# Retrieval layers: from gathered expert rows to streaming both expert tables through TensorE

## What is computed

```python
def one_block(xb):                                    # xb: 128 tokens
    q = (xb @ w_q).reshape(n, 8, 2, 128)
    s = jnp.einsum('thpk,pnk->thpn', q, sub_keys)     # 2 x 128 scores a head
    s_top, i_top = lax.top_k(s, 16)
    cand_s = s_top[:, :, 0, :, None] + s_top[:, :, 1, None, :]
    cand_i = i_top[:, :, 0, :, None] * 128 + i_top[:, :, 1, None, :]
    best_s, best_pos = lax.top_k(cand_s.reshape(n, 8, -1), 16)
    idx = jnp.take_along_axis(cand_i.reshape(n, 8, -1), best_pos, axis=-1)
    gate = jax.nn.softmax(best_s, axis=-1)
    act = jax.nn.gelu(jnp.einsum('thkd,td->thk', jnp.take(down, idx, axis=0), xb))
    return jnp.einsum('thk,thkd->td', gate * act, jnp.take(up, idx, axis=0))
```

## Time and profile before

| | us |
|---|---|
| median of 3 runs | 2358.21 (2356.95 to 2359.39) |
| span of the profiled execution | 2356.5 |
| retrieval layer 0 (about 209 to 892) | 683 |
| retrieval layer 1 with the pooling before it (892 to 1587) | 695 |
| rest after it | 769 |
| busy: PE 2048.2, DVE 1155.2, ACT 647.4, POOL 601.8 | |
| moved | 860.93 MB, of it 536.90 MB by gathers |

### The profile page before, as it was taken

One profiled execution on the slowest core, in us unless ns is written; L12 is line 12 of the kernel. 1 busy time (PEld: TensorE's weight loads), 2 busy tenths in 40 slices (PEclk: granted clock), 3 DMA queues, 4 the chain that ended last, 5 costly groups with the idle time before them and its releaser, 6 DMA issues.

```text
span 2356.5 us, 21481 instructions
## 1 busy us (share of the span) xinstructions
PE 2048.2 (87%) x7609; PEld 981.8 (42%) x7609; DVE 1155.2 (49%) x2857; ACT 647.4 (27%) x1813; POOL 601.8 (26%) x516
## 2 busy tenths in 40 slices
PE   7999998777777888998777777779999999999998
PEld 3455664232323336664223223334445544444443
DVE  2335766676667556766676667544534311111111
ACT  2242333332333222333332333332432210000001
POOL 0001344444444431344444444430000000000000
PEclk9999999999999998999999999999999999999999
DMA  9696999999999987999999999996313399999996
GB/s 391 252 423 246 407 417 420 420 416 422 406 420 413 409 347 293 406 420 421 421 420 417 412 421 412 407 396 262 119 57 135 160 402 427 428 426 428 427 427 262
DMA packets 98201, 860.93 MB, mean 365 GB/s; under 512 B 11406, under 2 KB 11534, under 8 KB 12844
## 3 DMA queue, kind: packets, MB, share of 16 engines
q0 software_dynamic: 73728, 536.90, 55.3%
q1 hardware_dynamic: 24364, 322.62, 32.9%
HBM read 858.44 MB, written 1.05 MB: 365 GB/s over the span
## 4 chain that ended last, share of the span: by engine, by line
PE 55%; DMA 29%; DVE 7%; ACT 4%; issue 3%; POOL 2%; POOLq 0%; SPq 0%; DVEq 0%; ACTq 0%
DMA arena<-in_experts,arena 16%; PE bank L2348 16%; PE bank L2012 15%; DMA ring<-in_experts,arena 9%; PE bank L2699 9%; PE bank L2745 4%; PE bank L2709 2%; PE bank L2116 2%; DVE arena L1479 2%; DMA arena<-in_w_up 2%; ACT arena L903 2%; POOL arena L696 1%; PE bank L2128 1%; POOL ring L696 1%; DVE ring L1479 1%
## 5 line engine op out<-in xcount | busy, mean ns | idle before, releaser
L2348 PE MATMUL bank<-arena 128*128 128x512 f32 x1040 | 486.3, 612 | 128.6 <-ACT arena L903 128.6
L2348 PE MATMUL bank<-ring,arena 128*128 128x512 f32 x1008 | 472.1, 612 | 116.5 <-ACT arena L903 116.4
L696 POOL DMA_INDIRECT arena<-in_experts,arena x260 | 299.8, 1153 | 638.2 <-PE bank L2348 331.7
L1479 DVE SCALAR_TENSOR_TENSOR arena<-arena,h 128x1024 f32<-128x1024 f32 x260 | 318.7, 1226 | 231.1 <-DMA arena<-in_experts,arena 230.1
L1479 DVE SCALAR_TENSOR_TENSOR ring<-ring,h 128x1024 f32<-128x1024 f32 x252 | 308.9, 1226 | 217.0 <-DMA ring<-in_experts,arena 216.4
L696 POOL DMA_INDIRECT ring<-in_experts,arena x252 | 301.8, 1198 | 329.5 <-PE bank L2348 288.4
L2348 PEld LDWEIGHTS bank<-arena 128*128 128x128 f32 x1040 | 191.2, 193 | 401.6 <-ACT arena L903 201.4
L2348 PEld LDWEIGHTS bank<-ring,arena 128*128 128x128 f32 x1008 | 185.5, 193 | 384.2 <-ACT arena L903 193.9
L894 ACT ACTIVATE arena<-arena 128x2 f32<-128x2 f32 x256 | 52.1, 203 | 838.5 <-DVE arena L1479 456.1
L2699 PE MATMUL bank<-ring,arena 128*64 128x512 f32 x768 | 223.4, 592 | 2.0 <-ACT arena L1096 1.2
L903 ACT ACTIVATE arena<-const,arena 128x128 f32<-128x128 f32 x512 | 177.6, 394 | 8.4
(11 more groups left out here) (430 smaller groups left out, 1811.8 us busy)
## 6 DMA issues: line engine op xcount, KB each, us to landing
ring<-in_w_gate SPq DMA_DIRECT2D x32, 2048.0 KB, 14.8
ring<-in_mod_w SPq DMA_DIRECT2D x20, 2048.0 KB, 11.8
arena<-in_w_up SPq DMA_DIRECT2D x16, 2048.0 KB, 20.9
arena<-in_w_down SPq DMA_DIRECT2D x16, 2048.0 KB, 15.8
ring<-in_w_up SPq DMA_DIRECT2D x16, 2048.0 KB, 16.4
ring<-in_w_down SPq DMA_DIRECT2D x16, 2048.0 KB, 11.5
ring<-in_w_in SPq DMA_DIRECT2D x9, 2048.0 KB, 7.3
ring<-in_peer_w_q SPq DMA_DIRECT2D x8, 2048.0 KB, 12.3
```

What stands on the lines that cost most here:

```text
L696: pool.indirect_dma_start(out=gslot(l, n), out_offset=None, in_=a["experts"], in_offset=bass.IndirectOffsetOnAxis(ap=idx_all[:, t, at:at + ...
L1479: ins = v.scalar_tensor_tensor(out=row, in0=row, scalar=1.0, in1=h[:, t], op0=ALU.mult, op1=ALU.mult, accum_out=act[:, t, HEAD * hh + k:HE ...
L2348: ins = pe.matmul(bank[2 * t + c][:, :], diag[:, PER * (j % 2) + k], row[:, 512 * c:512 * c + 512], start=j % (GROUPS // NT) == 0 and k == ...
```

## The change

Gathers, dot products and diagonals go. Each layer streams both tables whole, in pieces of 1 MB (`PIECE` x 128 partitions), with `down` laid out on the host so that it serves as stationary operand. For each key pair j the kept tile `kept(j)` is [i on partitions, 256 tokens]: PE makes all 128 x 256 products of experts (i, j) with all tokens (`products`, two keys a piece), and ACT writes their gelu there. DVE selects as before, but keeps i, j and the gate's exponent (`picks`); after both tiles' softmax PE turns them to [pick, token]. For each token then `one_hots` writes the one-hot of i (128 wide) and the one-hot of j times gate (64 wide, one half of the keys at a time) over the 128 picks, `spread_gates` multiplies them on PE into the gate matrix [i, j] of that token, 8 tokens a group, and `weigh` multiplies the kept tiles by it in place. `sums` multiplies the kept tiles, as stationary operand, with the streamed `up` rows into banks 0 to 3.

Only 112 of 128 kept tiles have room. So the order of a layer is: 56 pairs of products, with the queries of two heads each ahead of pairs 0, 4, 10 and 17 and the first half's 32 groups spread from pair 33; then 8 times one pair of sums and one of products; then the other sums, with the second half's groups behind pairs 8 to 31 and the last 8 pairs done first for tile 0 and then for tile 1. Pieces come through three places that free when PE has used the third before; the last five have places of their own. The late modulation rows (16 to 19) all go into layer 0, behind pairs 6, 9, 12 and 15, and the modulation totals behind the sums of pair 33 and on. Both tiles' norms stand ahead of a layer's first query, and the first three loads of `w_in_2` go out during layer 1's sums. `win` is kept apart from the constants, slots of later weights move (`MOE_RING`), and POOL has no work. The core of the diff:

```diff
-PER = 2
-GROUPS = PICKS * NT // PER
+TILE = 256
+KEPT = 112
+PAIR_TILES = KEYS // 2
+KEPT_PAIRS = KEPT // 2
+WRAPPED = PAIR_TILES - KEPT_PAIRS
+TAIL = 8
+STREAMS = 3
+PIECE = 2048
+QUERY_AT = {0: 0, 4: 1, 10: 2, 17: 3}
+ROW_AT_PAIR = {6: 16, 9: 17, 12: 18, 15: 19}
...
+EXP_AT = {29: 0, 32: 1}
+TURN_PICKS_AT = {31: 0, 34: 1}
+SPREAD = KEPT_PAIRS - 33
+GROUPS_AT = {33 + p: tuple(range(GROUPS * p // SPREAD, GROUPS * (p + 1) // SPREAD)) for p in range(SPREAD)}
+GROUPS_BEHIND = {p: tuple(range(4 * (p - WRAPPED) // 3, 4 * (p - WRAPPED + 1) // 3)) for p in range(WRAPPED, PAIR_TILES // 2)}
+TOTAL_AT = [{33 + n: n for n in range(10)}, {33: 10, 34: 11}]
...
-                    pool.indirect_dma_start(
-                        out=gslot(l, n), out_offset=None, in_=a["experts"],
-                        in_offset=bass.IndirectOffsetOnAxis(ap=idx_all[:, t, at:at + 1], axis=0)).then_inc(
-                        S[f"gathered{place_of(n)}"], 16)
...
+                def products_out(p):
+                    act_.wait_ge(S["piece_done"], done(l, "d", p))
+                    act_.activation(kept_pair(p), bank[4 + p % 2][:, :], ACT.Gelu_apprx_tanh).then_inc(S["s_ev"], 1)
...
+                def one_hots(half, g):
+                    n = group_no(l, half, g)
+                    at = slice(GROUP * g, GROUP * g + GROUP)
+                    keys = cst("iota")[:, HALF_KEYS * half:HALF_KEYS * half + HALF_KEYS]
+                    if half == 0 and g in (0, GROUPS // NT):
+                        v.wait_ge(S["picks_ev"], NT * l + g // (GROUPS // NT) + 1)
+                    if n >= 2:
+                        v.wait_ge(S["g_done"], n - 1)
+                    i_hot, j_hot = hot_i[:, n % 2], hot_j[:, n % 2]
+                    link(v.tensor_tensor(j_hot, bc(keys, 1, GROUP), bc(picksT[:, 1, at], 2, HALF_KEYS), ALU.is_equal))
+                    v.tensor_tensor(i_hot, bc(cst("iota"), 1, GROUP), bc(picksT[:, 0, at], 2, KEYS), ALU.is_equal)
+                    v.tensor_tensor(j_hot, j_hot, bc(picksT[:, 2, at], 2, HALF_KEYS), ALU.mult).then_inc(S["hot_made"], 1)
...
+                    for at, v0, width in runs:
+                        part = kept_run(v0, width)[:, :, GROUP * g:GROUP * g + GROUP]
+                        ins = v.tensor_tensor(part, part, gates_of_keys[:, at:at + width], ALU.mult)
+                    ins.then_inc(S["w_made"], 1)
...
+                def products(p):
+                    wait_piece(pe, l, "d", p)
+                    if p >= 2:
+                        pe.wait_ge(S["s_ev"], PAIR_TILES * l + p - 1)
+                    w = piece(l, "d", p).rearrange("p (j k n) -> p j k n", j=2, k=KT)
+                    for j in range(2):
+                        ins = accumulate(bank[4 + p % 2][:, TILE * j:TILE * j + TILE], [(w[:, j, q], hT[:, q, :]) for q in range(KT)])
+                    ins.then_inc(S["piece_done"], 1)
...
+                    for u in range(GROUP):
+                        ins = pe.matmul(bank[6 + n % 2][:, HALF_KEYS * u:HALF_KEYS * u + HALF_KEYS], hot_i[:, n % 2, u], hot_j[:, n % 2, u],
+                                        start=True, stop=True)
+                    ins.then_inc(S["g_done"], 1)
...
+                def sums(p, *tiles):
+                    w = piece(l, "u", p).rearrange("p (j d) -> p j d", j=2)
+                    for j in (2 * p, 2 * p + 1):
+                        for t in tiles:
+                            for c in range(2):
+                                ins = pe.matmul(bank[2 * t + c][:, :], tile(kept(j), t), w[:, j % 2, 512 * c:512 * c + 512],
+                                                start=j == 0, stop=j == KEYS - 1, skip_group_check=True)
+                    return ins
```

More of the change, by code:

```diff
@@ L75 @@
 INC = [(0, 512), (512, 512), (1024, 512), (1536, 256)]
+HEAD_QUERIES = [(256 * c, 256) for c in range(HEADS)]
 FIRST = (0, 2, 1, 3)
@@ L118 @@
 OPERANDS = {"tq1": 2, "pctx": 2, "tk1": 1, "ppool": 8, "tkc": 2, "th1": 1, "tq2": 4, "tgla": 3, "tkd": 2, "tgo": 2}
-SHADOW = 4
-STEPS = 15
-ROWS = 18
+STEPS = 14
 GAIN_ROW = 20
[L125 to L132, removed]
@@ L135, in selections @@
-def selections(l, m, head=1):
-    return 9 * l + (m + 1 if m else head) + 1
-PER = 2
-GROUPS = PICKS * NT // PER
-EARLY_SLOTS = 6
-def place_of(n):
[L149 to L159, removed]
+LATE_ROWS = (16, 17, 18, 19)
+TILE = 256
[3 more added lines that the diff above has]
+WRAPPED = PAIR_TILES - KEPT_PAIRS
@@ L482, in program @@
         mo = Carve(0)
-        w_moe = [ring[:, i, :] for i in range(RING)] + [mo(SLOT) for _ in range(2)]
-        moe_landed = w_landed + [S[f"moe_landed{i}"] for i in range(RING, 6)]
-        streamed = [16 * sum(load is not None and k == i for load, k in zip(loads, slots)) for i in range(RING)] + [0, 0]
+        MOE_RING = (2, 1, 0, 3)
+        w_moe = [ring[:, i, :] for i in MOE_RING] + [mo(SLOT) for _ in range(2)]
+        moe_landed = [w_landed[i] for i in MOE_RING] + arena_landed[3:5]
+        streamed = [16 * sum(load is not None and k == i for load, k in zip(loads, slots)) for i in MOE_RING] + [16 * 2, 16 * 2]
         hdn = mo(4, T)
@@ new lines, in peer @@
+                for n in range(HEADS):
+                    for step in range(STEPS):
+                        top_k(n, step)
+                    if l == 0 and n == 4:
+                        v.wait_ge(S["modp"], 4 + 20)
+                        v.tensor_tensor(mrows2, mrows1, bank[3][:, :], ALU.add).then_inc(S["rows_made"], 1)
+                gates(0)
+                for half in range(2):
+                    for g in range(GROUPS):
+                        one_hots(half, g)
+                        if (half, g) == (0, 1):
+                            gates(1)
+                        if g:
+                            weigh(half, g - 1)
+                    weigh(half, GROUPS - 1)
@@ new lines, in query @@
+                def query(hh):
+                    wait_piece(pe, l, "q", hh)
+                    if hh < 2:
+                        pe.wait_ge(S["turned_ev"], turned(tag, 4))
+                    else:
+                        pe.wait_ge(S["pq_ev"], HEADS * l + hh - 1)
+                    w = piece(l, "q", hh).rearrange("p (k n) -> p k n", k=KT)
+                    for half in range(2):
+                        ins = accumulate(bank[hh % 2][:, 256 * half:256 * half + 256],
+                                         [(tile(w[:, q], half), hT[:, q, :]) for q in range(KT)])
+                    ins.then_inc(S["piece_done"], 1)
@@ new lines, in scores @@
+                def scores(n):
+                    c, t = n // 2, n % 2
+                    if l == 0 and n == 1:
+                        pe.wait_ge(S["rows_made"], 2)
+                    pe.wait_ge(S["pq_ev"], HEADS * l + 2 * c + 2)
+                    if n >= 2:
+                        pe.wait_ge(S["ps_ev"], HEADS * l + n - 1)
+                    for s in range(4):
+                        ins = pe.matmul(tile(bank[6 + t], s), tile(qb[:, c % 2, s], t), keysT[:, l, s % 2], start=True, stop=True)
+                    ins.then_inc(S["ps"], 1)
```

807 lines of the change are left out of this document (334 added, 473 removed).

## The result

The changed kernel takes 3164.6 us in the median (3163.6 to 3166.5), 1.342 times the time before (95% interval 1.340 to 1.344). The forecast was 3172 us. The profiled span is 3163.9 us.

A forecast was written before the change was run, and what follows sets the result against it. The retrieval layers were taken as bound by 536.9 MB of gathers, PE about three quarters full behind. Terms: 209 + 1087 + 32 + 1071 + 771.5 = 3170.5 us of span, 1.7 more gives 3172 us; range 3130 to 3260.

The forecast's parts named there:

- What bounded the kernel before: Retrieval layers: bound by the 536.9 MB of gathers, with PE about three quarters full behind them.
- Layers: Both retrieval layers: PE work of 1061 us each, plus 21 or 5 us of extras and waits, 1087 and 1071 us.
- the allowed 5 us of waits: Each layer: short PE waits for the last weighing before each half's sums and behind the turning of the picks.
- The burst at the lower clock: Layer 0's first queries: first 32 records after idle took 6.32 us against 3.7 at the dense rate, so +2.5.
- The weighing of rule against row: Gate spreading's weight loads: skill's rule 0.107 us, 109 us a layer; profile row 0.114 us, 116 us a layer.
- DVE, ACT and POOL under PE: Retrieval layers: DVE hidden at 3.3 us a gate group, ACT's evictions 0.60 us each 6.9 us, POOL's removal frees nothing.
- The streams at nothing: Each layer's 143 MB of pieces, 343 us at 416 GB/s, costed at nothing under PE.
- The 13.7 us: Streamed pieces: with three places, each is issued two pieces of PE work, 13.7 us, ahead.
- loads that hide: Rival, gate spreading: weight load hides, 64 columns cost by columns alone, 57 us a layer, total 3054; chance 0.04.
- DVE's pace: Rival: DVE paces the spreading from 6.8 us a group; at 9.9 us, +195 a layer, total 3560; chance 0.06.
- starving streams: Rival: pieces starve PE from 6.9 us each; at 10.5 us, +490 a layer, total 4150; chance 0.03.
- The other side: Rival, products and sums: faster than before if a matmul costs under 0.62 of the price; half price 2093 us; chance 0.01.

The follow-up runs named there:

- Half the bytes: The kernel before with gathers of the up rows alone, 4 KB for each token and pick, dot products made with the up row: 2123 us, 0.900 times.
- The two one-hot kernels: The changed kernel with the 128-wide compare for i made twice in each group, 3164.0 us, and made five times, 3320.7 us.
- the halved loads: The changed kernel with one spreading matmul of 128 columns for two of 64, weight tiles loaded falling from 1024 to 512: 3050.2 us.
- doubled work: The changed kernel with the 128-wide compare made twice, 3164.0 us, or five times, 3320.7 us; with each 1 MB piece loaded twice in turn, 3277.8 us.

## Why the prediction was right

- What bounded the kernel before: right. Half the bytes gave 236 us, and PE's idle time before the sums fell to a fifth.
- Layers: 1087 and 1071 us forecast; 1085.6 (208.32 to 1293.94) and 1070.7 (1324.04 to 2394.74) measured. That they agree within 1.5 us is partly luck, terms that cancel. Products 6.91 us a pair among the sums and 6.96 among the spreading (6.87 forecast, +3 to +6 us a layer), sums 6.86 (6.90, -3), spreading 0.2175 a matmul (0.227, -5), and the allowed 5 us of waits was 2.6 of idle time. The burst at the lower clock, 2.7 us, which I had put ahead of the layer, lies in it.
- The weighing of rule against row came out for the rule: the load takes 0.109 us a record. The row's 0.114 was a reading slip: 3.65 us divided by 32 counts the whole of the last load. With that one's 0.192 us taken off it is (3.65 - 0.19) / 31 = 0.112.
- DVE, ACT and POOL under PE: right. The two one-hot kernels put DVE's limit between 4.3 and 8.1 us a group; it needs 3.06. ACT's slack wasn't tried; its 64 us of work in a layer left PE only the 1.6 us of waits at L767.
- The streams at nothing: right in size, but its reason was too broad. The 13.7 us cover how late a piece lands, and not how fast pieces follow each other. In the changed kernel SP waits for no landing (a megabyte lands in 4.8 us, one is wanted every 6.9), and that is fast enough. At one in 7.3 us, with the same places, it cost 113 us.
- Start of the first query 206.5 forecast, 208.3 measured. Between the layers 30.1 us from the last sum to the first query, with 2.9 more in the slow burst (85 records in 21.3 us, 18.4 at the dense rate), against 32. From the last sum to the end 769.2 us against 771.5: the z products started 1.8 us after the last sum where 2.4 were costed, and the rest ran 1.7 us shorter than before. Why wasn't tried. In the joins one reading was 0.1 off: 879.93 to 887.12 is 7.2 us, not 7.3.
- The rivals: loads that hide are excluded by the halved loads; DVE's pace and starving streams by doubled work. The other side is excluded at float32's price, and its mechanism is there: at about a quarter of it the change wins by 300 us. Its turning point, 0.62 of the price, wasn't tried. It let all 2158 us of PE work get cheaper; with the products and sums alone (2 x 881 us) the point would be at about 1 - 814 / 1762 = 0.54, an estimate from the forecast's own terms.

## What to carry to other kernels

Before trading bytes for matmuls, price the matmuls by columns and passes, and add them to the engine that stands second: in the kernel before that engine had 108 of 480 us free, and the change brought it 440 us a layer. A product that many weight tiles feed with few columns is priced by the tiles, so put two tokens' columns behind one tile where the layout allows it. A stream needs two checks, and places ahead answer only the first: does a piece land in time, and do pieces follow each other as fast as they are used where the consumer is fastest? A queue that waits for one landing before its next issue fails the second.

## What the runs showed of the hardware that I had not expected

- With 64 or 128 float32 columns behind a fresh tile of 128 columns a matmul costs the same 0.22 us (1.74 and 1.78 us for eight).
- The upper halves of float32 words, read in place with a step of two, stream at about a quarter of the float32 price (0.114 us for 256 columns, (1.99 - 0.17) / 16). No run has such halves stored densely, so what the step itself costs isn't shown.
- Pieces of 128 runs of 8 KB, 512 KB apart, came at 421 to 428 GB/s where PE waited for them.
- DMA at 254 GB/s in place of 142, the added part between places outside the core, didn't slow PE or DVE: 1015.2 and 1015.3 us for PE's same 4608 records, 926.8 us of DVE work in both.
- Two loads of 1 MB issued together, with a wait for a landing before the next two, went by in 7.3 to 7.5 us (281 GB/s). Without such waits the queue reached 428 GB/s.
- In the changed kernel the same wait of 0.87 us before the first sums was followed by a granted clock of 1.00 in layer 0 (16 records in 7.11 us from 727.12) and of 0.81 in layer 1 (8.76 us from 1834.85).
